# A two-block transformer forward pass: smaller level scaling, a 128-row rope product, another order at the start and in the convolution branch

## The reference

```python
# first block, layer 0: gated linear attention (GLA); layer 1: latent attention (MLA); a SwiGLU FFN after each
h = rmsnorm(x) * (1 + scale) + shift          # shift, scale, gate = silu(c) @ ada_w + ada_b
GLA:  log_a = log_sigmoid(glr @ w_gate + b) / 16;  o_t = sum_{s<=t} (q_t * k_s * exp(b_t - b_s)) v_s   # b = cumsum(log_a)
MLA:  s = q_nope @ k_nope.T + rope(q_rope) @ rope(k_rope).T;  p = softmax(causal(s * scale));  o = p @ v   # 8 heads, 128 + 64
# second block
p, a, g = split(h @ w_in + b_in)
y_pool = ((window_means(p, (2, 4, 8, 16)) - p) @ pool_w * pool_scale) @ pool_up
y_conv = silu(layernorm(depthwise_conv31(a1 * sigmoid(a2)) + dw_bias)) @ conv_out      # 512 channels, 31 taps, causal
x = x + gate * ((sigmoid(g1) * y_pool + sigmoid(g2) * y_conv) @ w_out)
x = x + gate * peer(h2)                       # top 16 of 16384 experts per head, done densely over all experts
return rmsnorm(x)
```

## Time and profile before

| | us |
|---|---|
| median of 3 runs | 3224.52 |
| lowest, highest | 3216.39, 3231.88 |
| the profiled execution | 3218.98 |
| its span | 3217.1 |
| PE busy | 3085.6 (96%) |
| POOL, DVE, ACT busy | 1775.1 (55%), 1608.6 (50%), 1151.3 (36%) |

### The profile page before, as it was taken

One profiled execution on the slowest core, in us unless ns is written; L12 is line 12 of the kernel. 1 busy time (PEld: TensorE's weight loads), 2 busy tenths in 40 slices (PEclk: granted clock), 3 DMA queues, 4 the chain that ended last, 5 costly groups with the idle time before them and its releaser, 6 DMA issues.

```text
span 3217.1 us, 44185 instructions
## 1 busy us (share of the span) xinstructions
PE 3085.6 (96%) x14632; PEld 2500.8 (78%) x14632; DVE 1608.6 (50%) x2785; ACT 1151.3 (36%) x1478; POOL 1775.1 (55%) x2040
## 2 busy tenths in 40 slices
PE   5988999998999999997999999999999999999998
PEld 3777788876568888775788888888888888888887
DVE  7873455322435552595316997444421444544443
ACT  4354322226342223433333234555543332333332
POOL 4833677645037766673545665444445666666663
PEclk8989999999999999998999999999999999999999
DMA  7511455522015554221323444555555655556552
GB/s 307 208 35 57 145 200 176 167 77 90 7 61 199 199 172 133 89 84 54 104 92 98 151 147 144 196 187 194 193 198 190 209 192 182 180 195 209 201 190 78
DMA packets 170201, 481.94 MB, mean 150 GB/s; under 512 B 15360, under 2 KB 48896, under 8 KB 168080
## 3 DMA queue, kind: packets, MB, share of 16 engines
q1 hardware_dynamic: 147680, 410.83, 39.1%
q10 hardware_dynamic: 22448, 70.14, 5.6%
HBM read 411.70 MB, written 69.21 MB: 149 GB/s over the span
## 4 chain that ended last, share of the span: by engine, by line
PE 52%; issue 23%; POOL 21%; DVE 2%; ACT 0%; DMA 0%; DVEq 0%; POOLq 0%; SPq 0%; ACTq 0%
PE ps L1626 49%; POOL w_lo L551 21%; PE pa L1626 4%; DVE s_acc L1420 1%; DMA e_g<-expert_act 0%; DVEq L1417 0%; DVE s_pb L1432 0%; DVE s_tmp L1471 0%; DVE mg_lo L1473 0%; ACT mg_hi L921 0%; DVE s_m L1469 0%; DVE x L1125 0%; POOLq L549 0%; POOLq L555 0%; DVE s_gl L1412 0%
## 5 line engine op out<-in xcount | busy, mean ns | idle before, releaser
L551 POOL TENSOR_TENSOR w_lo<-raw,w_hi 128x256 fp32r<-128x256 f32 x2036 | 1774.9, 903 | 1412.6 <-ACT w_hi L569 1411.3
L1626 PE MATMUL ps<-h_hi,w_hi 128*128 128x512 f32 x2392 | 944.8, 395 | 33.4 <-POOL w_lo L551 22.8
L1626 PE MATMUL ps<-h_hi,w_lo 128*128 128x512 f32 x2392 | 934.2, 391 | 0.0
L1626 PE MATMUL ps<-h_lo,w_hi 128*128 128x512 f32 x2392 | 914.5, 390 | 0.0
L569 ACT ACTIVATE w_hi<-raw 128x1024 fp32r<-128x1024 f32 x509 | 538.6, 1060 | 803.9 <-PE ps L1626 685.5
L1626 PEld LDWEIGHTS ps<-h_hi,w_hi 128*128 128x128 f32 x2392 | 450.6, 188 | 133.7 <-POOL w_lo L551 24.5
L1626 PEld LDWEIGHTS ps<-h_hi,w_lo 128*128 128x128 f32 x2392 | 450.6, 188 | 95.5
L1626 PEld LDWEIGHTS ps<-h_lo,w_hi 128*128 128x128 f32 x2392 | 450.4, 188 | 93.0 <-issue 1.7
L1626 PE MATMUL ps<-wa_hi,w_hi 128*128 128x512 f32 x1024 | 398.5, 389 | 0.5 <-DVE x L1590 0.5
L1626 PE MATMUL ps<-wa_hi,w_lo 128*128 128x512 f32 x1024 | 398.4, 389 | 0.0
L1626 PE MATMUL ps<-wa_lo,w_hi 128*128 128x512 f32 x1024 | 398.3, 389 | 0.0
(11 more groups left out here) (315 smaller groups left out, 3104.7 us busy)
## 6 DMA issues: line engine op xcount, KB each, us to landing
ada<-in_ada SPq DMA_DIRECT2D x144, 512.0 KB, 4.4
raw<-in_expert_u SPq DMA_DIRECT2D x128, 512.0 KB, 4.1
raw<-in_expert_v SPq DMA_DIRECT2D x128, 512.0 KB, 4.2
raw<-in_ffn_in SPq DMA_DIRECT2D x88, 512.0 KB, 3.5
expert_act<-g_act ACTq DMA_DIRECT2D x128, 256.0 KB, 4.2
gate_matrix<-w_st ACTq DMA_DIRECT2D x16, 2048.0 KB, 6.9
e_w<-gate_matrix SPq DMA_DIRECT2D x16, 2048.0 KB, 11.4
e_g<-expert_act SPq DMA_DIRECT2D x128, 256.0 KB, 7.5
```

What stands on the lines that cost most here:

```text
L551: last = nc.gpsimd.tensor_tensor(w_lo[:, k, c:c + 256], raw[:, k, c:c + 256], w_hi[:, k, c:c + 256].bitcast(F32), ALU.subtract)
L1626: return nc.tensor.matmul(out, a, b, start=start, stop=stop_)
```

## The change

- Start: weight blocks 0 to 3 are loaded ahead of x. ACT makes their w_hi ahead of the squares, DVE (not POOL) their w_lo, behind the first pair of modulation products; POOL's loop starts at block 4. `pe_first` takes four tiles. PE does eight products of constants before the sum of squares.
- Levels: k is scaled only in the first halves, q only in the second, into one joined row of 512 (`g_kq`, four buffers in place of two and two); PE uses it as both operands. The masked copy takes only the second halves (the diagonal item is as before).
- Attention: the rotated key rope is held twice on 128 rows, with the other head's 64 rows zero; the rope product takes 128 rows. Identity and mask of the causal product are bf16.
- Second block: DVE convolves one tile after another, the second half of a tile's taps interleaved with the first half of the next one's; pools 0 and 1 behind the convolution, 2 behind the mean's subtraction, 3 behind the last split. Mean behind tile 24, variance behind tile 25, mixes 0 and 1 behind all tiles, 2 and 3 amid `conv_out`, which now comes ahead of `pool_up`.

```diff
+WARM = 8
-    g_qs = ar("g_qs", 60 * K, [2, S])
-    g_ks = ar("g_ks", 64 * K, [2, S])
+    g_kq = ar("g_kq", 60 * K, [4, S])
-    m_kr = ar("m_kr", 56 * K, [S])
+    m_kr = [ar("m_kr0", 56 * K, [S]), at("m_kr1", rstd_off, [S])]
...
             if n == 1:
+                for m in range(RING):
+                    sp_raw(sp, m, A["gla_qk"][m - 1, :, :] if m else A["gla_glr"][:, :], 1024)
                 sp.dma_start(x[:, :, :], A["x"].rearrange("k p t -> p k t")).then_inc(ld_x, 16)
-            if n in (1, 3):
-                for m in (n - 1, n):
-                    sp_raw(sp, m, A["gla_qk"][m - 1, :, :] if m else A["gla_glr"][:, :], 1024)
...
-        with pool.Fori(0, last // RING) as i:
+        with pool.Fori(1, last // RING) as i:
...
+        if n == 0:
+            hi.upto(RING - 1)
         for k in range(DT):
...
-            if n == 0 and k == 0:
-                hi.upto(RING - 1)
...
-    Z_AT = 3
+    Z_AT = RING
...
-                act.wait_ge(kr_done, 1)
+                act.wait_ge(kr_done, 6)
...
-    MIX_AT, MEAN_AT, VAR_AT = (15, 16), 22, 24
+    MEAN_AT, VAR_AT = 24, 25
...
+        for g in range(4):
+            hi.upto(M0["conv_out"] + g // 2 + 3)
+            act.wait_ge(pw_mm, g + 1)
+            if g >= 2:
+                act.wait_ge(mix_done, 4)
+            own_a.link(act, nc.scalar.activation(s_pm[g], pa[:, 2 + g % 2, :], ACT.Copy, scale=col("pool_scale", g)))
+            nc.scalar.activation(pm_hi[:, g, :], s_pm[g], ACT.Copy).then_inc(pmh, 1)
...
+            if k == 0:
+                for m in range(RING):
+                    dve.wait_ge(hi_done, m + 1)
+                    nc.vector.tensor_tensor(w_lo[:, m, :], raw[:, m, :], w_hi[:, m, :].bitcast(F32), ALU.subtract)\
+                      .then_inc(lo_done, 1)
...
+        def halves(row, l, half):
+            s = GCH >> (l + 1)
+            return row.rearrange("p (n w) -> p n w", w=2 * s)[:, :, half * s:(half + 1) * s]
+
         def scaled(n):
             h, l, e = item_level(n)
             dve.wait_ge(lv_e, e + 1)
-            if e >= 2:
-                dve.wait_ge(lv_mm, (e - 2) // LEVELS * (LEVELS + 1) + (e - 2) % LEVELS + 1)
-            nc.vector.tensor_tensor(g_qs[:, e % 2, :], g_q[:, h, :], g_E[:, e % 2, :], ALU.mult)
-            nc.vector.tensor_tensor(g_ks[:, e % 2, :], g_k[:, h, :], g_E[:, e % 2, :], ALU.mult).then_inc(lv_q, 1)
+            if e >= 4:
+                dve.wait_ge(lv_mm, (e - 4) // LEVELS * (LEVELS + 1) + (e - 4) % LEVELS + 1)
+            for half, rows in enumerate((g_k, g_q)):
+                last = nc.vector.tensor_tensor(halves(g_kq[:, e % 4, :], l, half), halves(rows[:, h, :], l, half),
+                                               halves(g_E[:, e % 2, :], l, half), ALU.mult)
+            last.then_inc(lv_q, 1)
...
+            nc.vector.copy_predicated(halves(g_attn[:, h, :], l, 1).rearrange("p (c n) i -> p c n i", c=TT),
+                                      bc(halves(g_mask[:, l, :], l, 1), 1, TT),
+                                      halves(pa[:, n % 4, :], l, 1).rearrange("p (c n) i -> p c n i", c=TT)).then_inc(lv_cp, 1)
...
+        for a in range(2):
+            mine, other = slice(ROPE * a, ROPE * (a + 1)), slice(ROPE * (1 - a), ROPE * (2 - a))
+            v.memset(m_kr[a][other, :], 0.0).then_inc(kr_done, 1)
+            v.tensor_tensor(m_kr[a][mine, :], m_t[mine, :], m_sw[mine, :], ALU.add).then_inc(kr_done, 1)
+        v.tensor_copy(ident_b[:, :], ident).then_inc(kr_done, 1)
+        v.tensor_copy(causal_b[:, :], const("causal_t", P)).then_inc(kr_done, 1)
...
+        HALF = (CK - 1) // 2
+        done = [0]
+        def taps(*parts):
+            n, d = len(parts), done[0]
+            with dve.Fori(0, HALF) as i:
+                for j, (t, tap) in enumerate(parts):
+                    dve.wait_ge(conv_done, i * n + (d + j - (n - 1)))
+                    v.scalar_tensor_tensor(out=s_acc[:, t, :], in0=s_gl[:, t, bass.ds(i + tap, S)],
+                                           scalar=cols[:, bass.ds(i + (COLS["dw_kernel"] + t * CK + tap), 1)],
                                            in1=s_acc[:, t, :], op0=ALU.mult, op1=ALU.add).then_inc(conv_done, 1)
+            done[0] += n * HALF
+        begin(0)
+        taps((0, 1))
+        for t in range(1, 4):
+            begin(t)
+            taps((t - 1, 1 + HALF), (t, 1))
+        taps((3, 1 + HALF))
...
         if n == 0:
             pe.wait_ge(ld_c, 32)
+            for _ in range(WARM):
+                mm(pa[:, 1, :], ones, consts[:, 0:S], True, True)
...
-                    kk, qq = (g_ks[:, e % 2, w], g_qs[:, e % 2, w]) if l < LEVELS else (g_k[:, h, w], g_q[:, h, w])
+                    kk, qq = (g_kq[:, e % 4, w],) * 2 if l < LEVELS else (g_k[:, h, w], g_q[:, h, w])
...
-                mm(pa[:, s % 3, 0:n], m_qr[half, h // 2, q], m_kr[half, 0:n], False, False)
-                mm(pa[:, s % 3, n - P:n], ident, const("causal_t", P), False, True).then_inc(at_s, 1)
+                mm(pa[:, s % 3, 0:n], m_qr[:, h // 2, q], m_kr[h % 2][:, 0:n], False, False)
+                mm(pa[:, s % 3, n - P:n], ident_b[:, :], causal_b[:, :], False, True).then_inc(at_s, 1)
...
+        mix(0)
+        mix(1)
+        pe.wait_ge(cyl, 4)
+        branch("conv_out", cy_hi, cy_lo, {3: lambda: (mix(2), mix(3))})
         pe.wait_ge(pml, 4)
         branch("pool_up", pm_hi, pm_lo)
```

More of the change, by code:

```diff
@@ L73 @@
     ("ffn1_in", 44), ("ffn1_out", 24),
-    ("sec_in", 28), ("pool_up", 4), ("conv_out", 4), ("sec_out", 8),
+    ("sec_in", 28), ("conv_out", 4), ("pool_up", 4), ("sec_out", 8),
     ("query", 16), ("expert_u", 128), ("expert_v", 128),
@@ L82 @@
     ("ffn1_in", 44), ("ffn1_out", 8),
-    ("sec_a", 8), ("sec_p", 4), ("sec_g", 16), ("pool_up", 8), ("conv_out", 8), ("sec_out", 8),
+    ("sec_a", 8), ("sec_p", 4), ("sec_g", 16), ("conv_out", 8), ("pool_up", 8), ("sec_out", 8),
     ("query", 16), ("expert_u", 128), ("expert_v", 128),
@@ L495, in sp_program @@
         sp_ffn(sp, 1)
-        for name in ("sec_in", "pool_up", "conv_out", "sec_out"):
+        for name in ("sec_in", "conv_out", "pool_up", "sec_out"):
             sp_segment(sp, name, A[name], 1024)
@@ L1424, in dve_second, with begin @@
-        convolve(0, 2)
-        for g, w in enumerate(WINDOWS):
+        HALF = (CK - 1) // 2
+        done = [0]
+        def begin(t):
+            dve.wait_ge(tile_free, T0["sec_a"] + 2 * t + 2)
+            v.tensor_tensor(s_gl[:, t, PAD:], s_a1[:, t, :], s_sig[t % 3][:, :], ALU.mult).then_inc(glu_done, 1)
+            dve.wait_ge(glu_done, t + 1)
+            v.tensor_scalar(s_acc[:, t, :], s_gl[:, t, 0:S], col("dw_kernel", t * CK), col("dw_bias", t),
+                            ALU.mult, ALU.add).then_inc(conv_done, 1)
+            done[0] += 1
@@ L1439, in dve_second @@
             v.tensor_tensor(s_mix[:, g, 0:PPAD], mean0, s_p[:, g, PPAD:2 * PPAD], ALU.subtract).then_inc(mix_done, 1)
-        convolve(2, 4)
-        for g in range(4):
-            dve.wait_ge(pmh, g + 1)
-            v.tensor_tensor(pm_lo[:, g, :], s_pm[g], pm_hi[:, g, :].bitcast(F32), ALU.subtract).then_inc(pml, 1)
+        pool(0, WINDOWS[0])
+        pool(1, WINDOWS[1])
+        assert done[0] == 4 * CK
         dve.wait_ge(conv_done, 4 * CK)
@@ L1449, in dve_second @@
                                    op0=ALU.mult, op1=ALU.add).then_inc(cx, 1)
+        pool(2, WINDOWS[2])
         dve.wait_ge(crs, 1)
@@ L1457, in dve_second, with conv_out @@
             v.tensor_tensor(cy_lo[:, t, :], s_acc[:, t, :], cy_hi[:, t, :].bitcast(F32), ALU.subtract).then_inc(cyl, 1)
+        pool(3, WINDOWS[3])
+        def conv_out(a, b):
+            for k in range(a, b):
+                dve.wait_ge(blk_done, M0["conv_out"] + k // 2 + 1)
+                v.tensor_tensor(s_sg[:, DT + k, :], s_sg[:, DT + k, :], ps[:, (T0["conv_out"] + k) % RING, :], ALU.mult)\
+                  .then_inc(tile_free, 1)
+        dve.wait_ge(tile_free, T0["conv_out"])
+        conv_out(0, 4)
+        for g in range(4):
+            dve.wait_ge(pmh, g + 1)
+            v.tensor_tensor(pm_lo[:, g, :], s_pm[g], pm_hi[:, g, :].bitcast(F32), ALU.subtract).then_inc(pml, 1)
+        conv_out(4, DT)
         T = T0["pool_up"]
@@ L1886, in pe_mla @@
         pe.wait_ge(qr_done, MH // 2)
-        pe.wait_ge(kr_done, 1)
+        pe.wait_ge(kr_done, 6)
         n_it = MH * TT
@@ L1948, in pe_second, with branch @@
                 last.then_inc(cvar, 1)
-        def branch(name, hi, lo):
+        def branch(name, hi, lo, after=None):
             for k in range(DT):
@@ L1959, in branch @@
                     last.then_inc(blk_done, 1)
+                if after and k in after:
+                    after[k]()
+        mix(0)
+        mix(1)
+        pe.wait_ge(cyl, 4)
+        branch("conv_out", cy_hi, cy_lo, {3: lambda: (mix(2), mix(3))})
         pe.wait_ge(pml, 4)
         branch("pool_up", pm_hi, pm_lo)
-        pe.wait_ge(cyl, 4)
-        branch("conv_out", cy_hi, cy_lo)
```

52 lines of the change are left out of this document (14 added, 38 removed).

## The result

| | before | after |
|---|---|---|
| median of the runs, us | 3228.20 (4 runs, 3216.39 to 3234.13) | 3186.73 (4 runs, 3185.55 to 3187.87) |
| ratio, 95% interval | | 0.9876 [0.9846, 0.9906] |
| span of the profiled execution | 3217.1 | 3183.5 |
| mean granted clock | 0.983 | 0.990 |

What follows compares the result with a forecast made beforehand. TensorE, hardly ever idle, was taken as the bound. Start 4.5, levels 8.5, attention 12 and convolution 4 sum to 29: 3219.0 to 3190, set at 3193 because the earlier runs' median lay above the profiled execution; range 3175 to 3212.

Steps and rivals of the forecast that it cites:

- done at about 53: Start: TensorE finishes its first four tiles at about 53 us, the eighth h_lo coming at about 51.
- its 4.55: Start: w_hi and w_lo of the fifth block take 1.1 + 4.3 to 6.8 us, with 4.55 called the middle.
- What I named as the cost: Start: the gate product stands one tile later, behind the fifth tile of 5.5 us, and comes at 64.5 to 66.9.
- the middle of 1.75: Levels: an item behind the weight tiles takes 1.75 us, between 1.65 and about 1.9 at low clock; before 2.41.
- The 2.0 per head that is saved: Attention: shorter rope and causal products, 0.3 and 0.2 us a step, save 2.0 us per head.
- the 0.65 that turns into waiting: Attention: of the saving per head, 0.65 us becomes waiting for VectorE's chain, leaving 1.35 for each of 8 heads.
- 1.2 more at the first head: Attention: the first head, which runs at the low clock, gains 1.2 us beyond the 10.8 of all heads.
- The rival in which the clock falls with less work: Attention: TensorE's clock falls, 7 us more per low-clock head, 3248 us with all eight; chance 0.04.
- Both new waits: Convolution: TensorE waits 3.1 us before the variance and 6.3 us before conv_out for the last cy_lo.
- less 1.5 for low clock behind two gaps: Convolution: 1.5 us of the 5.5 gained is lost to low clock behind two gaps, leaving 4.

Runs made afterwards that it cites:

- e3: The changed kernel with the gate product directly behind the first four tiles and ScalarE's absolute values behind the fourth: 3180.04 us, 6.7 below the changed kernel.
- e5: The changed kernel with the copies of every level over full rows again, scaling still at half rows: 3189.21 us, 2.5 above the changed kernel.
- e4: The changed kernel with ScalarE's squares ahead of tile 25's evacuation, and rstd, SiLU and splits ahead of tile 26's: 3175.34 us, 11.4 below the changed kernel.
- e1: The kernel before with the zeroed 128-row rope operand alone, causal product kept in fp32: 3205.16 us, 0.9944 of before.

## Why the prediction was right, step by step

**Start: mis-sized, 1.35 and not 4.5.** Its first half came out to the tenth (first weight product 30.4, last h_lo 50.9). The step that failed is "done at about 53": it lets TensorE finish 2 us behind the last h_lo. The modulation products run three blocks ahead of the scaling, so behind the fifth block VectorE has none left and scales every 1.33 us and not every 4.13, while TensorE needs 12 products, 2.72 us, for each row block. It began the fifth at 46.22 and was done at 57.66. The step behind it, from there to the fifth tile, took 5.1 us, and the forecast has 5.4 to 7.9 (its 4.55 is not the middle of 4.3 to 6.8, and from 53 on its terms add to 63.9 to 66.4). With the fifth tile at the low clock (62.8 to 68.3) the gate product is 3.06 later and not 2 earlier. That the first level was 0.8 earlier all the same is VectorE's doing: 15 of its last twenty-four modulation products lay beside GpSimd, at 1.68, and not 20, which is 2.7 of the 3.9 us between the two. What I named as the cost, the fifth tile ahead of the gate product, was the cost: e3 took it away and gained 6.7 us.

**Levels: right, mis-sized below, 10.95 and not 8.5.** Half-row operations were 0.34 (I took 0.35), copies too. The term that was mis-sized is the middle of 1.75: with turns at the low clock I came to it, and an item took 1.60, at the high clock throughout. What a read of PSUM with gaps costs, the copy shows. With runs of 4 values or more it takes 0.41 to 0.45, with runs of two and of one 0.72 to 0.74, as much as the full row's 0.73; behind the weight tiles the scaling, which reads and writes only SBUF in the same pattern, stays at 0.41 to 0.43 at all of them. The Trainium skill (SBUF — State Buffer, "Door 1: The DMA port swizzle") says that any non-contiguous access pattern in PSUM slows matmuls down significantly, and has no price for a copy of VectorE; here the copy is slow at two levels of seven. The Trainium skill (Advanced Engine Details and Errata, "Memory Cachelines") asks, for PSUM, that every two consecutive elements be contiguous for best throughput. Taken for this copy, runs of two would be quick; here they are not, at 0.72. The copy reads a mask in SBUF with the same gaps beside PSUM, so which operand costs this isn't shown.

**Attention: right in each price, too low in sum, 16.39 and not 12.** 0.86, 0.86, 0.06, a head of 9.13 for 9.1: all as worked out. The 2.0 per head that is saved was 1.89, and the 0.65 that turns into waiting was 0.55 (0.22 to 0.77). The step that was mis-sized is "1.2 more at the first head": with the shorter steps the low clock behind the first score lasted 3.4 us and not 10.2, and a second low stretch of 3.4 us at the last head of before is missing. Half of the 10.2 us that the clock was low less is 5.1, most of the 5.7 that the stretch gained beyond 8 x 1.34. The rival in which the clock falls with less work went the other way: TensorE's mean granted clock rose, here and over the whole span.

**Between the stages: 2.85 that I had not, and that isn't the change's.** It lies in the rest of GLA: from the first transpose to the first product of GLA's output tiles 52.74 before, 49.44 after. With the start or the levels alone it is 49.44 too, with the convolution alone 50.86 and with the attention alone 51.94; before had two low stretches there, at 261 and 268. No edit touches this stretch, and with the whole change but for the copy (e5) it is 51.92, with one low stretch of 6.8 us: it is the clock, which differs there from execution to execution.

**Convolution: half of it, 1.91 and not 4.** The taps were right: end of the chain 151.3 behind the stage's start by my numbers, 150.2 measured; single taps 1.15 and not 1.33, pairs 33.97, 30.60 and 30.57 for 31. Both new waits were right too, 2.85 for 3.1 and 6.39 for 6.3. The step that was mis-sized is "less 1.5 for low clock behind two gaps". The mean took 6.58 for 5.3, the variance 5.40 for 3.5, conv_out's first 48 products 13.05 for 10.9: 5.3 us. I also took both waits for the price of the new order. e4 has the same order of taps and tiles and neither wait: they come when the variance follows one tile behind the mean and squares and rstd still stand in ScalarE's queue behind the next tile's evacuation, which the change left as it was.

## What to carry to other kernels

When a change makes one chain earlier, follow it to the next engine that is asked: 10 us at the first weight product became 1.4, because the product that VectorE waited for stood behind one more tile, and moving that product into the gap gave back 6.7. A small operation that a critical chain needs belongs ahead of the tile evacuation in its engine's queue, not behind it: four squares, rstd and four SiLU cost 11.4 us that way. And a stage's gain can be more than its shorter operations: in the attention some 5 of 16.4 us are shorter low stretches of TensorE's clock. Fewer gaps they are not, since the wait per head rose from 0.22 to 0.77; what shortened them isn't shown.

## What the runs showed of the hardware that I had not expected

- The same wait of 2.15 us before the attention was followed by 10.2, 10.2, 10.3 and 23.9 us at the low clock in four profiles of the same attention code, and by 0 to 3.4 with the shorter steps. In no profile was the clock low in the 20 us ahead of it.
- A predicated copy of 256 values a row out of PSUM takes 0.41 to 0.45 in runs of 4 to 64 values and 0.72 to 0.74 in runs of two or one. Its mask and its result in SBUF have the same gaps.
- A float32 product of 128 x 512 that takes 0.86 between products on 128 rows takes 0.95 in front of one on 64 rows, and that one 1.06 to the next on 128. With a zeroed operand of 128 rows all are 0.86 (e1).
- A modulation product of VectorE is 1.15 from start to start with GpSimd silent and 1.68 with GpSimd at work.
